# Seven gate tiles of the odd input projection move into the latent state-space stage of a two-block sequence kernel

## The reference

```python
z, xbc, dt = split(h @ w_in, (2048, 3072, 64))          # 41 tiles of 128 columns
xs, bm, cm = split(silu(dwconv1d(xbc, conv_w, conv_b)), (2048, 512, 512))
dt = softplus(dt + dt_bias)
# context only hands its final state over; the latent tokens are two chunks of 128
cum = cumsum(dt * A)
w   = exp(cum[t] - cum[s], s <= t) * (cc @ bc.T) * dt[s]
y   = w @ x + exp(cum) * (cc @ state)                    # 32 heads, forward and backward
y   = (y + d_skip * x) * silu(z)                         # z is the gate: 16 tiles
y   = rmsnorm over each of 4 groups of 512 channels
out = y @ w_out
```

## Time and profile before

| | |
|---|---|
| median of three runs | 1795.35 us |
| profiled execution, its own time | 1799.98 us |
| its span | 1798.3 us |
| TensorE busy | 1698.9 us, 94% |
| VectorE busy | 1345.1 us, 75% |
| ScalarE busy | 847.9 us, 47% |
| GpSimd busy | 55.4 us, 3% |
| DMA | 245.90 MB, mean 137 GB/s |

### The profile page before, as it was taken

How to read it: one execution, slowest core, us unless ns; L and a number is a source line. 1 busy time by engine, 2 the same in 40 slices (tenths; PEclk the granted TensorE clock), 3 DMA queues, 4 the chain that set the end, 5 groups by cost and what they waited for, 6 DMA issues and landing times. The chain is left out here.

```text
span 1798.3 us, 26476 instructions
## 1 busy us (share of the span) xinstructions
PE 1698.9 (94%) x10222; PEld 1448.4 (81%) x10222; DVE 1345.1 (75%) x2521; ACT 847.9 (47%) x1476; POOL 55.4 (3%) x113
## 2 busy tenths in 40 slices
PE   4899999898999999999999998999998999999997
PEld 3788877676888888877788766988897988989997
DVE  6678884876999999968984678699965555765594
ACT  2623335635544443245553565333344467665541
POOL 0910000000000000000000000000000000000000
PEclk9999999999999999999999999999999999999998
DMA  8343441031222226733553333554555454344452
GB/s 318 119 152 125 127 132 51 29 112 70 94 94 94 94 94 220 236 129 129 174 167 119 117 100 113 182 158 152 153 188 178 147 172 151 129 127 134 140 166 81
DMA packets 70150, 245.90 MB, mean 137 GB/s; under 512 B 7951, under 2 KB 9480, under 8 KB 69768
## 3 DMA queue, kind: packets, MB, share of 16 engines
q1 hardware_dynamic: 68024, 241.52, 41.5%
q10 hardware_dynamic: 2000, 2.69, 0.5%
HBM read 242.80 MB, written 1.11 MB: 136 GB/s over the span
## 5 line engine op out<-in xcount | busy, mean ns | idle before, releaser
L462 PE MATMUL banks<-m,weights_high 128*128 128x256 f32 (+1 forms) x4336 | 1045.0, 334 | 31.3 <-DVE weights_low L498 24.7
L462 PEld LDWEIGHTS banks<-m,weights_high 128*128 128x128 f32 x4336 | 737.2, 192 | 124.9 <-issue 23.3
L462 PE MATMUL banks<-m,weights_low 128*128 128x256 f32 (+1 forms) x2168 | 716.8, 331 | 0.0
L498 DVE TENSOR_TENSOR weights_low<-weight_ring,weights_high 128x1024 fp32r<-128x1024 f32 x293 | 355.5, 1222 | 226.8 <-ACT weights_high L493 225.9
L462 PEld LDWEIGHTS banks<-m,weights_low 128*128 128x128 f32 x2168 | 415.4, 192 | 37.5
L493 ACT ACTIVATE weights_high<-weight_ring 128x1024 fp32r<-128x1024 f32 x293 | 309.0, 1057 | 233.2 <-PE banks L462 152.9
L630 DVE SCALAR_TENSOR_TENSOR m<-m,columns 128x189 f32<-128x189 f32 (+4 forms) x856 | 321.8, 450 | 24.9 <-ACT m L570 24.7
L769 DVE SCALAR_TENSOR_TENSOR m<-weight_ring,m 128x1024 bf16<-128x1024 f32 x184 | 225.1, 1223 | 18.0 <-DMA weight_ring<-in_weights 12.2
L569 ACT ACTIVATE m<-banks,columns 128x512 f32<-128x512 f32 (+1 forms) x120 | 83.2, 693 | 303.8 <-PE banks L462 303.7
L462 PE MATMUL banks<-m,weight_ring 128*128 128x256 f32 x704 | 152.1, 379 | 0.0
L462 PEld LDWEIGHTS banks<-m,weight_ring 128*128 128x128 f32 x704 | 133.7, 190 | 18.1
(11 more groups left out here) (395 smaller groups left out, 1580.2 us busy)
## 6 DMA issues: line engine op xcount, KB each, us to landing
weight_ring<-in_weights SPq DMA_DIRECT2D x433, 512.0 KB, 3.7
m<-entering SPq DMA_DIRECT2D x32, 256.0 KB, 3.3
x<-in_tokens SPq DMA_DIRECT2D x1, 2048.0 KB, 14.3
m<-in_cmp_w SPq DMA_DIRECT2D x1, 2048.0 KB, 7.4
m<-in_cond SPq DMA_DIRECT2D x2, 512.0 KB, 4.9
out<-x ACTq DMA_DIRECT2D x8, 128.0 KB, 1.9
columns<-in_columns SPq DMA_DIRECT2D x1, 633.0 KB
m<-in_rg_w ACTq DMA_DIRECT2D x1, 512.0 KB, 3.5
```

What stands on the lines that cost most here:

```text
L462: mm = pe.matmul(out, lhsT, rhs, start=p.start and i == 0, stop=p.stop and i == len(passes) - 1)
L498: dve.tensor_tensor(w_lo[:, g % PARTS, :], K.ring[:, PLACE[PRODUCT_BLOCKS[g]] % RING, :], w_hi[:, g % PARTS, :].bitcast(F32), ALU.subtract ...
```

## The change

The last seven gate items leave the projection and become the items of a second `run_products`, which is now the latent stage. The steps of the latent stage, unchanged in their work, run beside these products in a class `LatentSteps`.

- The projection ends with gate tile 8 (`Z_LATE = 9`), without the idle matmuls behind it. Its activations stay in memory for the second call.
- The new call has one bank for its products (`banks=1`), bank 0. The spreads move to banks 1 to 4.
- TensorE halves each pair: the first half is spread and state product, the second the products with x. `places` gives each half a tick: one half behind each of a gate item's tiles 0 to 6 and three behind tile 7; the first six places are left empty. `half` of TensorE now gets a fraction where it got a whole number.
- ScalarE and VectorE run pair i at the whole tick below its place (`slot`).
- The late gate items are emptied by two instructions, tanh(z/2) and z/2, since silu(z) = z/2 (1 + tanh(z/2)); VectorE's `add` takes one instruction more for each of them. The table set for tanh and exp is loaded at the stage's start.
- The sums of squares are copied out, and logarithm and root are taken behind the last pair, for three groups at once and then the fourth, with the logarithm's table set loaded before them.
- The loads of the entering decays are issued by GpSimd instead of SyncE.

```diff
@@ _run_products
-                    beside.half("tensor", pe, 2 * e + (k + 1) * 2 * len(r) // len(r[0].products) - 1)
+                    beside.half("tensor", pe, 2 * e + (k + 1) * 2 * len(r) / len(r[0].products) - 1)
@@ ssd_projection
-    for c in range(KI):
+    for c in range(Z_LATE):
...
-                 acc_slots=SSD_ACC, fill=16, tail=13)
+                 acc_slots=SSD_ACC, fill=16)
@@ ssd_latent
+    for c in range(Z_LATE, KI):
+        def empty(act, bank, c=c):
+            act.activation(zs[:, c, :], bank[:, 0:LAT], ACT.Tanh, scale=0.5)
+            if c >= Z_LATE + steps.NZ:
+                act.wait_ge(*steps.added.at(c - steps.NZ + 1))
+            return act.activation(steps.half_z[:, c % steps.NZ, :], bank[:, 0:LAT], ACT.Copy, scale=0.5)
...
+    run_products(K, rounds, beside=steps, banks=1)
@@ LatentSteps
-    LONG, SHORT, OUT, SIDE = 0, 2, 5, 7
+    LONG, SHORT, OUT, SIDE = 1, 3, 5, 7
+    AT_END = 3
...
+        places = [2 * (e + (k + 1) / KD) - 1 for e in range(KI - Z_LATE) for k in range(KD)
+                  for _ in range(self.AT_END if k == KD - 1 else 1)]
+        self.places = places[-2 * len(self.pairs):]
...
+    def slot(self, i):
+        at = int(self.place(i) // 1)
+        return self.end - 3 if at == self.end - 2 else at
...
             for i, (g, q, d) in enumerate(pairs):          # TensorE
+                yield self.place(i)
                 if i + 2 < n_pairs:
                     pe.wait_ge(*exped.at(i + 1))
                     spread(i + 2)
...
+                yield self.place(i, 1)
                 pe.wait_ge(*weighted.at(i + 1))
...
             for i, (g, q, d) in enumerate(pairs):          # ScalarE, VectorE
+                yield self.slot(i)
...
+                    link(dve.tensor_tensor(xl[:, c, :], xl[:, c, :], self.half_z[:, c % self.NZ, :], ALU.mult))
+                    ins = dve.scalar_tensor_tensor(xl[:, c, :], zs[:, c, :], 1.0, xl[:, c, :], ALU.add, ALU.mult)
...
+        yield self.end
+        act.preload_act_table_set(LOG_EXP)
+        store_sum(SG - 2)
...
+        root(slice(0, SG - 1), rstd[:, 0:SG - 1, :])
+        act.wait_ge(*self.summed.at(SG))
+        root(slice(SG - 1, SG), K.bank[:, self.SIDE:self.SIDE + 1, 0:LAT])
```

More of the change, by code:

```diff
@@ L59 @@
 LOG_EXP = "natural_log_exp_and_others"
+EXP_TANH = "exp_and_others"
 SEGMENTS = [
@@ L194, in __init__ @@
         self.entering_stored = count("entering_decays_stored")
+        self.entered = [count(f"entering_decays_landed{i}") for i in range(4)]
         self.release = {}
@@ L2130, in odd_mixer @@
         with K.activations(KD * T):
-            ssd_projection(K, zs, xl, xc, bt, ct, dcol, rows, state, (modulator, blocks[:late]))
-        with K.scope():
-            normed = ssd_latent(K, xl, zs, bt, ct, dcol, rows, state)
+            with K.scope():
+                ssd_projection(K, zs, xl, xc, bt, ct, dcol, rows, state, (modulator, blocks[:late]))
+            with K.scope():
+                normed = ssd_latent(K, xl, zs, bt, ct, dcol, rows, state)
         with K.activations(KI * LAT):
@@ L2165, in ssd_projection @@
     run_products(K, first_together(rounds), mods, prepare=Normalise(K, 0, "mix_g1", (1, 0, 8)), beside=steps, banks=4,
-                 acc_slots=SSD_ACC, fill=16, tail=13)
-SSD_ACC = 6
+                 acc_slots=SSD_ACC, fill=16)
+SSD_ACC, Z_LATE = 6, 9
 WEND, SOURCE = 0, 2
@@ L2325, in ssd_latent @@
 def ssd_latent(K, xl, zs, bt, ct, dcol, rows, state):
-    nc = K.nc
-    NW, NE, PAIRS = 3, 4, 8
-    LONG, SHORT, OUT, SIDE = 0, 2, 5, 7
-    FAR = 1e30
-    xt, cb = K.take(2, LT, 512), K.take(2, 2, 3 * P)
-    W, read = K.take(NW, 2, 3 * P), K.take(2, 2, LAT)
-    sq, pick = K.take(8, LAT), K.take(64, dtype=F32R)
-    ident, ahead = K.take(P, dtype=BF16), K.take(2, 2, P, dtype=BF16)
-    rstd = zs[:, 0:SG, :]
-    entering, landed = K.take(NE, 2, LAT), K.counts(NE)
-    (spreads, exped, weighted, scaled, used, picks, scored, masked, turned, kept, added, squared, summed, logged,
-     vector_step) = K.counts(15)
@@ L2550, in ssd_latent @@
-    K.stage_end()
-    return lambda dve, c: dve.scalar_tensor_tensor(xl[:, c, :], xl[:, c, :], K.col("ssd_norm", c), rstd[:, c // 4, :],
-                                                   ALU.mult, ALU.mult)
+    steps = LatentSteps(K, xl, zs, bt, ct, dcol, rows, state)
+    rounds = []
+    for c in range(Z_LATE, KI):
[4 more added lines that the diff above has]
+            return act.activation(steps.half_z[:, c % steps.NZ, :], bank[:, 0:LAT], ACT.Copy, scale=0.5)
+        rounds.append([Item(tile_products(FIRST_TILE["ssd_in"] + (25 + c) * KD, KD,
+                                          lambda k: K.h_parts(T, k, CTX, T), LAT), empty)])
```

410 lines of the change are left out of this document (224 added, 186 removed).

## The result

The changed kernel takes 1810.82 us (median of 5 executions, 1804.78 to 1812.87) where the kernel before takes 1795.35: a ratio of 1.0079 with a 95% interval of 1.0058 to 1.0100, so slower by 15.5 us. The profiled execution of that second set ran at a mean granted clock of 0.65 and took 2425.39 us; it is left out of that ratio and of all that follows. The forecast was +6.35 us, 1801.7, in a range up to 1808: the sign was right, the size too small by more than half.

The account below looks back on a forecast made before the run. TensorE was taken to bound the stage, with short waits at its edges. Terms -4.9 - 0.4 - 0.35 - 0.2 + 6.15 + 1.3 + 4.75 = +6.35 us on 1795.35 gave 1801.7 us, range 1793.5 to 1808.

Parts of the forecast that it names:

- the sign: Whole kernel: forecast slower, +6.35 us; slower given 0.59, within 0.2% 0.29, faster 0.12.
- The waits inside the loop: Latent loop: TensorE's short waits should go as added products give ScalarE and VectorE slack, -4.9 us (0 to -5.3).
- The item ends: Behind gate items' last products TensorE waits 1.31 us for exponentials queued behind the emptying: +6.15 us (+3 to +8).
- The last end: Behind the last gate item TensorE waits 2.8 us where the last two pairs wait 1.5: +1.3 us (0 to +2.5).
- VectorE, ScalarE and the loads: In the loop, their added work fits idle time and loads from GpSimd run ahead: 0 us beside the places named.
- the clock at the barrier: Stage's start: 3.40 us at the lower clock, costing 1.7 us, taken to stay as it was; no change priced.
- The two terms that I did price: Opening: barrier earlier without 13 idle matmuls, -0.4 us; first tile's three matmuls inside the wait for masks, -0.35 us.
- form switches: In 25 pairs a tile parts the narrow halves, two array-form changes of 0.19 us together: +4.75 us (0 to +9.5).
- The clock at the end: Stage's end: only roots leaving the chain and a longer last `add` were priced, -0.2 us (-1.0 to +1.0).
- the clock falls at the item ends: Rival: 1.3 us waits bring the lower clock at each of five item ends, +14.9 us, 1810.2 us; chance 0.10.
- Already in it: Rival: form-switch drains hide under weight loads, so only item ends cost, +1.6 us, 1797.0 us; chance 0.25.
- tiles fill: Rival: tiles' matmuls go into time a pair wastes, 32 pairs giving 10.9 us back, -4.5 us, 1790.8 us; chance 0.12.

Follow-up runs that it names:

- that second set: Changed kernel, unaltered, executed again among the experiments: ratio 1.0077 (1.0063 to 1.0090) to the kernel before.
- e1: Changed kernel with the 13 idle matmuls behind the projection put back: 1810.21 us, ratio 1.0076 to the kernel before.
- b1: Kernel before with only the 13 idle matmuls behind the projection left out: ratio 1.0020 to the kernel before.
- b2: Kernel before with one idle full-width matmul between the 64-column halves of each of 32 pairs: ratio 1.0059 to the kernel before.
- b3: Kernel before with one idle full-width matmul ahead of the full-width spread in each of 32 pairs: ratio 1.0022 to the kernel before.
- e5: e3 with both halves of a pair at one place, so no tile stands between 64-column products: ratio 1.0017 to the kernel before.
- e2: Changed kernel with idle matmuls set into TensorE's last waits at the stage's end: ratio 1.0083 to the kernel before.
- e3: Changed kernel with ScalarE doing a pair's exponentials ahead of the item's tanh and copy at item ends: ratio 1.0051 to the kernel before.

## Why the prediction was wrong

**Right.** The sign. The waits inside the loop went. The item ends: a wait of 1.19 us at four of them and of 0.60 at the one with the `turn`, for 1.31 and 0.4 less; from the moment at which TensorE could start (1081.71 + 0.89 for its second half) it is 1.26. The last end: 2.76 us for 2.8. VectorE, ScalarE and the loads: no wait of TensorE for a landing, the 32 loads took 3.4 us from GpSimd, 3.3 from SyncE:

```profile
m<-entering POOLq DMA_DIRECT2D x32, 256.0 KB, 3.4
```

**The step that failed: the clock at the barrier.** I took "the change leaves these waits and I leave that cost" and so put the clock at nothing. The two terms that I did price came as forecast: the first spread starts 4.21 us behind the cut (977.15 to 981.36) where it was 4.59 (999.26 to 1003.85), and the first tile stands inside that wait. What leaving out the 13 idle matmuls took away besides was the work that kept the lower level to 3.4 us; without them it lasts 13.65. Forecast -0.75 for the opening, measured +3.8 to +4.0. Of that 2.6 to 2.7 us are the idle matmuls' (changed less e1), 3.0 in b1. The remaining 1.3 is e1's, whose 3.4 us of low clock fall into the opening's tiles and not, as before, into pair 0. That pair took 3.65 us before, from spread to spread, where 2.06 is the pace:

```profile
1009.38 0.51 PE L2386 MATMUL banks<-m 128*128 128x256 f32 x1
1013.03 0.38 PE L2386 MATMUL banks<-m 128*128 128x256 f32 x1
```

So 1.6 us of the opening's excess has only moved there from the loop, and the clock at the barrier costs 3.0 us net: the opening is 4.6 over its forecast in the profile with full clock in the end, less these 1.6.

**The size of the form switches, the larger miss.** I read 0.10 us for leaving the narrow form, assumed 0.09 for entering it and took 0.19 for both; the pairs of b2 against b3 give 0.34, those of the changed kernel against e5 0.35. A tile between halves takes 0.70 us where 0.54 was forecast (0.35 and the switches), a tile between pairs 0.35 as forecast:

```profile
1086.38 0.28 PE L2435 MATMUL banks<-m 128*128 128x256 f32 x1
1087.11 0.65 PE L2463 MATMUL banks<-m 128*64 128x256 f32 x4
1087.69 0.50 PE L464 MATMUL banks<-m,weights_high 128*128 128x256 f32 x2
1088.03 0.28 PE L464 MATMUL banks<-m,weights_low 128*128 128x256 f32 x1
1088.24 0.65 PE L2469 MATMUL banks<-m 128*64 128x256 f32 x4
1088.72 0.39 PE L2471 MATMUL banks<-m 128*64 128x128 f32 x4
1089.04 0.50 PE L464 MATMUL banks<-m,weights_high 128*128 128x256 f32 x2
1089.50 0.28 PE L2435 MATMUL banks<-m 128*128 128x256 f32 x1
```

State product to tile is 0.58 us, 0.10 over the 0.48 to another narrow product: that is the 0.10 which I had read. But the full-width tile behind narrow products is itself slower: 0.46 us (1089.04 to 1089.50) where a tile among tiles takes 0.35. So leaving costs another 0.10, hidden in the step after the one that I looked at; between pairs nothing more is paid for it, since a spread behind narrow products bears the same 0.10 (0.83 us to its state product, and 0.73 behind a tile: 1086.38 to 1087.11). The tile between the halves takes 0.55 to the second half, and the second half's first step is 0.48 where it was 0.43: 0.10 and 0.05 for entering.

The 25 tiles between halves make 8.9 us of switches where 4.75 was forecast, +4.1. Against that the ends cost 1.2 us less than forecast (7.15 and the 0.62 left, of 6.15 and 2.8), and 1.6 us of low clock left the loop. That gives +1.3 of the 2.2 by which 9.5 exceeds 7.3; the rest, 0.9, would be less recovered from the old waits than the 6.4 us that I had counted (4.9, and the last two pairs' 1.5), which no run measured apart, though b3's matmuls covered only 4.4 us of them. All parts together, 4.1 + 3.0 - 1.2 + 0.9 + 0.5 in the end, are the 7.3 us by which the stage's +13.7 at full clock in the end exceeds +6.35.

"TensorEngine Tiling (Array Packing)" of the Trainium skill, section Key Properties, says that a change of mode drains TensorE; the trace agrees, at 0.34 to 0.35 us for there and back.

**The clock at the end.** Forecast -0.2; at full clock it is +0.3. In the first profile the lower level adds 3.0 us there, 0.9 in the loop, and about 1.3 in ssd_out's opening (3.40 us at 0.63). The rival "the clock falls at the item ends" had the right mechanism at the wrong place: the clock fell at none of the five ends, in the opening always, behind the last item in two of three profiles. That its 1810.2 us lies 0.6 from the measured 1810.8 is luck: it priced five falls at item ends, and none came. "TensorE: Matmul & The Clock Gate" of the Trainium skill, section HAM oscillation, warns of idle gaps between bursts of matmuls, and its Part 1, on the clock gate, says that what a kernel sees of it varies from run to run. The traces agree with the second (0.61, 0.74 and 1.00 in one kernel's ends); of the first they show that gaps of 2.81 and 2.76 us, shorter than those that the page warns of, can be enough.

**The other rivals.** "Already in it" and "tiles fill" are refuted by b2: the form is paid for, and nothing of the added matmul is hidden. A pair with two tiles takes 3.12 us (1086.38 to 1089.50), 0.17 over the forecast 2.95.

## What to carry to other kernels

Idle matmuls ahead of a barrier are not waste if a thin opening follows: before counting their removal as a gain, price the next stage's TensorE work at half clock. When pieces of another stage are dealt into a stage that packs the array narrowly, deal them where the form changes anyway; same tiles, same count, 7 us here. And a wait that a new emptying brings into an engine's order is often gone by issuing what TensorE waits for ahead of it, though the next wait on the chain (here the last add behind weight parts) takes a share of the gain.

## What the runs showed of the hardware

A stop of 2.81 us at a barrier ahead of a thin opening (waits of 0.65, 1.37 and 0.69 us in it) was followed by some 13.65 us at 1.2 GHz in each of the three profiles of the changed kernel and in those of e2, e3 and e5, and a stop of 4.04 us in b1 by as much; with 13 idle matmuls ahead of the barrier, and 0.30 us of idle there, the low stretch was 3.4 us, and the opening's mean clock 0.88 where it had been 0.58 to 0.61. The same code with the same waits of 2.76 and 1.2 to 1.4 us ran its end at a clock of 0.61, 0.74 and 1.00 in three executions. Going from 64-column to full-width products and back costs 0.34 to 0.35 us, of which only 0.10 shows in the step from narrow products to the next full-width one.
